# Shared keys of a two-block network: high weights over both parts of the activations in one 512-column product

## The chip, the cores and the metric

The kernel runs on one core of one Trainium2 chip. The metric is the device time of a run in microseconds (us), lower is better. Names of engines: PE is TensorE (matrix products; PEld is its weight load), DVE is VectorE, ACT is ScalarE, POOL is GpSimd, SP issues most DMAs. PSUM is the memory that PE writes to, eight banks of 512 fp32 columns in each of 128 partitions; SBUF is the memory that the engines work from.

## The reference, cut to what matters

Two blocks of two layers each run over 256 tokens of width 1024. The change touches one step of the second block, which makes the keys and values that a later attention layer uses:

```python
def _shared_kv(x, kv_norm, w_kv, k_gain):
    kv = (_rms(x, kv_norm) @ w_kv).reshape(bsz, seq, 2, B_GROUPS, B_HEADS, B_HEAD_DIM)
    k = _rms(kv[:, :, 0], k_gain[:, None, :])     # 3 groups x 16 heads x 64
    v = kv[:, :, 1]
```

That is a product of [256 x 1024] with [1024 x 6144], of which 3072 columns are keys, with a second normalisation over each head's 64 channels, and 3072 are values. All is fp32.

## The kernel before, in words

**Products in two parts.** Every fp32 weight and activation is split into a high and a low part of a type that PE multiplies in one pass (fp32r). ACT copies the weight to `hi` (L339), and DVE or POOL subtracts to get `lo` (L345). Activations are held as `xh` and `xl`. `product` (L393 to L397) adds three matmuls into PSUM: high weight x high activation, high x low, low x high.

**Chunks.** Weights come in chunks of 1024 x 256 through a ring of three buffers, so `hi` of chunk n can be written only when the products of chunk n-3 are done. Stages follow one another in one list (`PLAN`). The stage here is `kv`, between the feed-forward blocks `glu1` and `glu2`. It has 24 chunks, which alternate: chunk 2k holds keys and chunk 2k+1 values (k from 0 to 11). I call chunks 2k and 2k+1 pair k. `lo` of key chunks is made by DVE and `lo` of value chunks by POOL.

**A key chunk** is 2 halves of 128 output channels x 8 slices of the contraction x 3 matmuls of 256 columns (the tokens), 48 matmuls, all into one bank. **A value chunk** has the parts the other way round (activations are loaded, weights stream), 48 matmuls of 256 columns as well.

**What happens to the keys of pair k.** In this order: DVE multiplies the bank by the first normalisation's factors (L2268, raises `lin`). ACT squares (L2322, raises `sqr`). PE averages the squares over each head by an fp32 matmul with a constant (`mean`, L2224), placed between the two halves of value chunk 2k+1 for k > 0. ACT takes Ln (L2285) and Exp (L2288), each behind a table load. DVE scales the keys (L2260).

**The orders on the engines are written out by hand.** An engine works strictly down its list:

- ACT, turn k: square k, `hi` of 2k+3, Ln k, Exp k, the values of pair k out of their bank (L2293), `hi` of 2k+4, square k+1.
- DVE, turn k: `lo` of 2k+2, the keys of pair k out of their bank (L2268), scale keys k (L2260); for k = 6, 7, 8 also one addition for a table of position biases (L2277). Then `lo` of 2k+4.
- PE, pair k: key chunk, first half of the value chunk, mean k, second half; for k = 6, 7, 8 then a small matmul for the bias table (L2245).

At the end of the stage `glu2` needs new `xh` and `xl` (L1060 on ACT, L947 on DVE), since its gains differ. DVE makes `lo` of `glu2`'s second chunk first, then `xl`. PE's first matmul of `glu2` waits for the first two tiles of `xl`.

Of the kernel before, what the change touches and what calls it, by code (L numbers as in the profile page):

```python
# [132 lines left out]
def build(nc, A, out, plan=PLAN):  # L133

    ctx = ExitStack()
    with ctx:
        names = [0]

        def sb(name, shape, dt=F32):
            return ctx.enter_context(nc.sbuf_tensor(name, shape, dt))  # L140

        def sem(name):
            return ctx.enter_context(nc.semaphore(name))
# [3 lines left out]
        x = sb("x", [P, KT, T])  # L147
        hi = [sb(f"hi{i}", [P, 2048], F32R) for i in range(RING)]
        lo = [sb(f"lo{i}", [P, 2048], F32R) for i in range(RING)]
        xh = sb("xh", [P, KT, T], F32R)  # L150
        xl = sb("xl", [P, KT, T], F32R)
        gh = sb("gh", [P, 2, 2, T], F32R)
        gl = sb("gl", [P, 2, 2, T], F32R)
        cum_r, sel_r = sb("cum_r", [P, T], F32R), sb("sel_r", [P, 16], F32R)
# [6 lines left out]
        mean_d = sb("mean_d", [P, P])  # L161
        zero16 = sb("zero16", [1, P], BF16)
        ident = sb("ident", [P, P])
        bank = [ctx.enter_context(nc.psum_tensor(f"bank{i}", [P, 512], F32)) for i in range(8)]

        arena_at = nc.sbuf_base
        arena = sb("arena", [P, ARENA])
# [4 lines left out]
        def take(*shape, at=None):  # L172

            n = int(np.prod(shape))
            o = top[0] if at is None else at
            top[0] = o + n
            assert top[0] <= ARENA, top[0]
            v = arena[:, o:o + n]
            if len(shape) == 2:
                return v.rearrange("p (a b) -> p a b", a=shape[0])  # L180
            if len(shape) == 3:
                return v.rearrange("p (a b c) -> p a b c", a=shape[0], b=shape[1])
            return v
# [206 lines left out]
        def slot(n, width=CW, of=None):  # L390
            return (ring if of is None else of)[n % RING][:, 0:KT * width].rearrange("p (k n) -> p k n", k=KT)
# [285 lines left out]
        def pe_stats(pe, b):  # L677

            st = info[b]["st"]
            pe.wait_ge(ssq_new, st)  # L680
            nc.tensor.matmul(bank[7][:, 0:T], mean_d[:, :], ssq[:, :], start=True, stop=True)
            nc.tensor.matmul(bank[7][:, T:T + 1], ssq[:, 0:P], mean_d[:, 0:1], start=True, stop=True)
            nc.tensor.matmul(bank[7][:, T + 1:T + 2], ssq[:, P:T], mean_d[:, 0:1], start=True,
                             stop=True).then_inc(stat_new, 1)
            if b == FINAL:
                pe.wait_ge(fin_dve, 3)
                nc.tensor.matmul(bank[6][:, 0:T], mean_d[:, :], fin_q, start=True, stop=True)
                nc.tensor.matmul(bank[6][:, T:T + 1], fin_q[:, 0:P], mean_d[:, 0:1], start=True, stop=True)
                nc.tensor.matmul(bank[6][:, T + 1:T + 2], fin_q[:, P:T], mean_d[:, 0:1], start=True,
                                 stop=True).then_inc(fin_stat, 1)  # L690

        def pe_half(pe, n, B, mode, h, width=CW, tiles=None, acts=None, freed=False, ks=range(KT)):

# [1508 lines left out]
        def make_kv():  # L2202
# [4 lines left out]
            n0 = info["kv"]["c0"]  # L2207
            lin, sqr, mean_ok, log_ok, rec_ok, done = (sem("kv_" + k) for k in ("lin", "sqr", "mean", "log", "rec", "done"))
            small_in, rel_mm, rel_ok, v_ok = sem("kv_small_in"), sem("kv_rel_mm"), sem("kv_rel_ok"), sem("kv_v")


            def pe_part(pe):
                for c in range(24):
                    k, value = divmod(c, 2)
                    if c >= 4:
                        pe.wait_ge(v_ok if value else lin, k - 1)

                    def mean():
                        if k == 0:
                            pe.wait_ge(const_in, 16)  # L2220
                        pe.wait_ge(sqr, k + 1)
                        if k >= 2:
                            pe.wait_ge(log_ok, k - 1)
                        nc.tensor.matmul(bank[4 + k % 2][:, :], C["block64"][:, :], tmp_sq[k % 2], start=True,  # L2224
                                         stop=True).then_inc(mean_ok, 1)

                    early = value and k > 0
                    if c == 0:
                        pe_first_chunk(pe, "kv", bank[0])
                    for h in range(2 if c else 0):  # L2230
                        if h and early:
                            mean()
                        pe_half(pe, n0 + c, bank[c % 4], "tm" if value else "fm", h, freed=c == 23)
                    if c == 0:
                        pe_stats(pe, "kv")
                    if value:
                        if not early:
                            mean()
                        if 6 <= k < 9:
                            g = k - 6  # L2240
                            if g == 0:
                                pe.wait_ge(small_in, 16 * 3)
                            if g == 2:
                                pe.wait_ge(rel_ok, 1)
                            nc.tensor.matmul(bank[6 + g % 2][0:16, 0:384], RB[0:32, 16 * g:16 * g + 16],  # L2245
                                             HOT[0:32, g, :], start=True, stop=True).then_inc(rel_mm, 1)
                pe.wait_ge(v_ok, 11)
                pe.wait_ge(lin, 12)
                pe.wait_ge(rel_ok, 3)
# [12 lines left out]
            def dve_part(dve):  # L2262
                rs2 = rs_b[:, :].unsqueeze(1).broadcast_to([P, 2, T])
                for k in range(12):
                    lo_until(dve, n0 + 2 * k + 2)
                    dve.wait_ge(chunk_mul, n0 + 2 * k + 1)
                    two = DK[:, 2 * k:2 * k + 2, :]
                    nc.vector.tensor_tensor(two, bank[2 * k % 4][:, :].rearrange("p (e t) -> p e t", e=2), rs2,  # L2268
                                            ALU.mult).then_inc(lin, 1)
                    lo_until(dve, n0 + 2 * k + 3)  # L2270
                    if k < 11:
                        scale_keys(dve, k)
                    if 6 <= k < 9:
                        g = k - 6
                        dve.wait_ge(small_in, 16 * 3)
                        dve.wait_ge(rel_mm, g + 1)
                        nc.vector.tensor_tensor(RV[0:16, g, :], bank[6 + g % 2][0:16, 0:384], RM[0:16, g, :],  # L2277
                                                ALU.add).then_inc(rel_ok, 1)
                lo_until(dve, n0 + 25)

# [9 lines left out]
            def values_out(act, k):  # L2290
                act.wait_ge(chunk_mul, n0 + 2 * k + 2)
                for t in range(2):
                    last = nc.scalar.activation(DV[:, t, k * CW:(k + 1) * CW],  # L2293
                                                bank[(2 * k + 1) % 4][:, t * CW:(t + 1) * CW], ACT.Copy, scale=rs_c[:, t:t + 1])
                last.then_inc(v_ok, 1)

            def finish(act, k):
# [471 lines left out]
```

## Time and profile before

| | us |
|---|---|
| median of 3 runs | 1966.73 |
| lowest, highest | 1966.43, 1970.43 |
| span of the profiled execution, first to last instruction | 1963.3 |
| PE busy | 1906.0 (97%) |
| DVE busy | 1198.9 (61%) |
| ACT busy | 979.1 (50%) |
| POOL busy | 120.6 (6%) |

For the profiled execution the page gives the span and no other time; that lies 3.4 us below the median of the three timed runs. In a row of the timeline the first number is the start in us from the beginning of the span, the second the busy time, and brackets hold the time the engine was idle before it and who ended that. PE's matmuls are pipelined, so their starts tell their pace, not their durations. A busy share of 97% is a share over the whole span, and tells nothing on what would end a wait in one stage.

### The profile page before, as it was taken

What the parts mean: (1) busy time and instruction counts of PE and PEld (TensorE: products, weight loads), DVE (VectorE), ACT (ScalarE), POOL (GpSimd) and SP (SyncE); (2) the same over time, 40 slices, a digit from 0 to 9 for tenths busy, and PEclk for the clock granted to TensorE, in tenths of its full rate; (3) what the DMA queues carried; (4) which work ended last, traced back from release to release, by engine and by line L of the source; (5) the groups of instructions that cost most, each with busy time, mean ns of one, the idle gap of its engine ahead of it and who ended that gap; (6) DMA issues with size and microseconds to landing.
All of it is one profiled execution on the core that took longest, in us unless ns stands there. A gap on an engine that the chain in (4) does not pass through costs nothing.

```text
span 1963.3 us, 36765 instructions
## 1 busy us (share of the span) xinstructions
PE 1906.0 (97%) x15832; PEld 1834.1 (93%) x15832; DVE 1198.9 (61%) x1396; ACT 979.1 (50%) x1158; POOL 120.6 (6%) x54
## 2 busy tenths in 40 slices
PE   7999999999999999999999999999999998999999
PEld 7879999898999999999999999899999987779999
DVE  6677666755766775558667555533655566646554
ACT  6365444545544453345455444776534356655433
POOL 0000000010000000000000000333000021220000
PEclk9999999999999999999999999999999999999999
DMA  6315444432545445554335555454555446435552
GB/s 264 129 47 182 184 181 154 182 132 106 188 177 188 176 155 178 185 182 162 108 108 198 188 178 176 161 174 156 194 174 189 172 167 174 109 96 189 190 173 105
DMA packets 57980, 320.57 MB, mean 163 GB/s; under 512 B 6144, under 2 KB 19536, under 8 KB 20752
## 3 DMA queue, kind: packets, MB, share of 16 engines
q1 hardware_dynamic: 55968, 314.76, 46.6%
q10 hardware_dynamic: 1904, 4.24, 0.6%
q8 instruction: 84, 1.38, 0.3%
q14 instruction: 24, 0.20, 0.0%
HBM read 317.85 MB, written 1.12 MB: 162 GB/s over the span
## 4 chain that ended last, share of the span: by engine, by line
PE 85%; DVE 8%; ACT 4%; issue 2%; DMA 0%; SPq 0%; ACTq 0%; DVEq 0%
PE bank L395 26%; PE bank L396 25%; PE bank L397 25%; DVE lo L345 3%; ACT hi L339 2%; PE bank L462 1%; DVE xl L947 1%; PE bank L1884 1%; PE bank L499 1%; PE bank L2224 1%; DVE x L957 1%; PE bank L2389 1%; DMA ring<-in_ev_in 0%; PE bank L480 0%; DVE arena L555 0%
## 5 line engine op out<-in xcount | busy, mean ns | idle before, releaser
L395 PE MATMUL bank<-xh,hi 128*128 128x256 f32 x2960 | 848.7, 287 | 19.8 <-DVE lo L368 10.1
L396 PE MATMUL bank<-xl,hi 128*128 128x256 f32 x2960 | 841.4, 284 | 0.0
L397 PE MATMUL bank<-xh,lo 128*128 128x256 f32 x2960 | 841.2, 284 | 0.0
L345 DVE TENSOR_TENSOR lo<-ring,hi 128x2048 fp32r<-128x2048 f32 x272 | 619.6, 2283 | 306.2 <-ACT hi L339 305.9
L339 ACT ACTIVATE hi<-ring 128x2048 fp32r<-128x2048 f32 x290 | 549.2, 1898 | 424.7 <-PE bank L397 419.0
L395 PEld LDWEIGHTS bank<-xh,hi 128*128 128x128 f32 x2960 | 570.5, 193 | 29.3 <-issue 23.9
L396 PEld LDWEIGHTS bank<-xl,hi 128*128 128x128 f32 x2960 | 570.6, 193 | 1.8 <-issue 1.5
L397 PEld LDWEIGHTS bank<-xh,lo 128*128 128x128 f32 x2960 | 570.5, 193 | 0.3
L395 PE MATMUL bank<-gh,hi 128*128 128x256 f32 x1056 | 299.1, 283 | 2.1 <-DVE gl L877 2.1
L396 PE MATMUL bank<-gl,hi 128*128 128x256 f32 x1056 | 298.9, 283 | 0.0
L397 PE MATMUL bank<-gh,lo 128*128 128x256 f32 x1056 | 298.8, 283 | 0.0
L395 PEld LDWEIGHTS bank<-gh,hi 128*128 128x128 f32 x1056 | 202.7, 192 | 2.5 <-DVE gl L877 2.5
L397 PEld LDWEIGHTS bank<-gh,lo 128*128 128x128 f32 x1056 | 202.7, 192 | 0.0
L396 PEld LDWEIGHTS bank<-gl,hi 128*128 128x128 f32 x1056 | 202.7, 192 | 0.0
L345 POOL TENSOR_TENSOR lo<-ring,hi 128x2048 fp32r<-128x2048 f32 x18 | 84.7, 4707 | 1506.1 <-ACT hi L339 1506.1
L395 PE MATMUL bank<-hi,xh 128*128 128x256 f32 x368 | 110.0, 299 | 0.9 <-DVE arena L1669 0.8
L396 PE MATMUL bank<-lo,xh 128*128 128x256 f32 x368 | 104.0, 283 | 0.0
L397 PE MATMUL bank<-hi,xl 128*128 128x256 f32 x368 | 104.0, 283 | 0.0
L908 ACT ACTIVATE gh<-arena 128x512 fp32r<-128x512 f32 x66 | 41.7, 632 | 121.1 <-DVE arena L874 121.1
L845 DVE TENSOR_TENSOR arena<-bank,rs_b 128x512 f32<-128x512 f32 x66 | 45.6, 691 | 88.2 <-PE bank L397 88.0
L555 DVE TENSOR_TENSOR arena<-bank,arena 128x384 f32<-128x384 f32 x80 | 40.8, 551 | 65.9 <-PE bank L482 33.1
L395 PE MATMUL bank<-dk_r,hi 128*128 128x256 f32 x256 | 74.4, 291 | 2.3 <-DVE dk_r L594 2.0
(266 smaller groups left out, 1942.6 us busy)
## 6 DMA issues: line engine op xcount, KB each, us to landing
ring<-in_ffn_in SPq DMA_DIRECT2D x132, 1024.0 KB, 4.9
ring<-in_ffn_out SPq DMA_DIRECT2D x66, 1024.0 KB, 4.8
ring<-in_kv SPq DMA_DIRECT2D x24, 1024.0 KB, 4.9
ring<-in_hg_in SPq DMA_DIRECT2D x16, 1024.0 KB, 4.9
ring<-in_od_in SPq DMA_DIRECT2D x12, 1024.0 KB, 4.8
ring<-in_dq SPq DMA_DIRECT2D x12, 1024.0 KB, 4.9
ring<-in_ev_in SPq DMA_DIRECT2D x10, 1024.0 KB, 6.7
arena<-rel_rows SPq DMA_DIRECT2D x24, 256.0 KB, 3.7
```

The lines of the kernel that those rows point to most:

```text
L339: nc.scalar.activation(hi[n % RING][:, 0:words[n]], ring[n % RING][:, 0:words[n]], ACT.Copy).then_inc(hi_ok, 1)
L345: ns.tensor_tensor(lo[n % RING][:, 0:w], ring[n % RING][:, 0:w], hi[n % RING][:, 0:w].bitcast(F32), ALU.subtract).then_inc(lo_ok[lo_by[n]], 1)
L395: nc.tensor.matmul(out_, lh, rh, start=start, stop=False, **kw)
L396: nc.tensor.matmul(out_, lh, rl, start=False, stop=False, **kw)
L397: return nc.tensor.matmul(out_, ll, rh, start=False, stop=stop, **kw)
L462: last = nc.tensor.matmul(soft_bank(w, e)[:, c0:c1], sub["q"][:, q0:q0 + P], sub["k"][:, 0:k1], start=True, stop=one)
L499: nc.tensor.matmul(out[e][:, 0:T], un["subs"][e][g]["v"][0], s.pt[w % 2][e][:, 0:T], start=un["first"] and g == 0, stop=False, skip_group_ ...
L555: nc.vector.tensor_tensor(a[e][:, g, :], soft_bank(w, e)[:, 0:384], un["subs"][e][g]["add"], ALU.add).then_inc(soft_sem["masked"], 1)
L845: nc.vector.tensor_tensor(dst, ga, rs2, ALU.mult).then_inc(ff_read, 1)
L908: nc.scalar.activation(gh[:, par, :, :], ff_g[:, par, :, :], ACT.Copy).then_inc(gh_ok, 1)
L947: last = nc.vector.scalar_tensor_tensor(xl[:, t, :], x[:, t, :], gain_of(b, t), xh[:, t, :].bitcast(F32), ALU.mult, ALU.subtract)
L957: nc.vector.scalar_tensor_tensor(xs, y, scale, xs, ALU.mult, ALU.add).then_inc(x_new, 1)
```

## The change

In key chunks 1 to 11 (k > 0) the high weight is no longer run over `xh` and `xl` in two matmuls of 256 columns, but once over both, which now lie side by side in one tensor `xhl`. The result fills a whole bank of 512 columns: the first half is high x high (to which low x high is added), the second is high x low. Each of the two channel halves takes a bank of its own. DVE then copies the second halves to SBUF, adds the first halves to them, and multiplies the sum by the factors as before. Key chunk 0 and all value chunks keep their products. Banks are dealt out anew: keys in banks 0 and 1 (k even) or 6 and 7 (k odd), values in 2 and 3, and the bias table shares banks 4 and 5 with the means, for which PE's waits on `log_ok` and `rel_ok` are added. A wait on `std_new` stands ahead of chunk 2, since banks 6 and 7 are then written for the first time after the statistics in bank 7 were read.

```diff
-        xh = sb("xh", [P, KT, T], F32R)
-        xl = sb("xl", [P, KT, T], F32R)
+        xhl = sb("xhl", [P, 2, KT, T], F32R)
+        xh, xl = xhl[:, 0, :, :], xhl[:, 1, :, :]
...
+        def product_beside(B, lh, ll, both, start, stop):
+            nc.tensor.matmul(B[:, :].rearrange("p (l t) -> p l t", l=2), lh, both, start=start, stop=False)
+            return nc.tensor.matmul(B[:, 0:T], ll, both[:, 0, :], start=False, stop=stop)
...
+            low_half = take(2, T)
+            def rel_bank(g):
+                return bank[4 + (g + 1) % 2]
+            def key_banks(k):
+                return (0, 1) if k % 2 == 0 else (6, 7)
+            def key_halves(k):
+                a, b = key_banks(k)
+                two = banks[:, a:b + 1, :].rearrange("p e (l t) -> p l e t", l=2)
+                return two[:, 0, :, :], two[:, 1, :, :]
 
             def pe_part(pe):
                 for c in range(24):
...
+                    if c == 2:
+                        pe.wait_ge(std_new, info["kv"]["st"])
...
+                        if 7 <= k < 10:
+                            pe.wait_ge(rel_ok, k - 6)
...
-                        pe_half(pe, n0 + c, bank[c % 4], "tm" if value else "fm", h, freed=c == 23)
+                        if value:
+                            pe_half(pe, n0 + c, bank[2 + k % 2], "tm", h, freed=c == 23)
+                            continue
+                        if h == 0:
+                            wait_split(pe, n0 + c)
+                        wh, wl = slot(n0 + c, of=hi), slot(n0 + c, of=lo)
+                        e = slice(h * P, (h + 1) * P)
+                        for i in range(KT):
+                            last = product_beside(bank[key_banks(k)[h]], wh[:, i, e], wl[:, i, e], xhl[:, :, i, :],
+                                                  i == 0, i == KT - 1)
+                        if h == 1:
+                            last.then_inc(chunk_mul, 1)
...
-                            if g == 2:
-                                pe.wait_ge(rel_ok, 1)
+                            pe.wait_ge(log_ok, k)
...
                     two = DK[:, 2 * k:2 * k + 2, :]
-                    nc.vector.tensor_tensor(two, bank[2 * k % 4][:, :].rearrange("p (e t) -> p e t", e=2), rs2,
-                                            ALU.mult).then_inc(lin, 1)
+                    if k == 0:
+                        y = bank[0][:, :].rearrange("p (e t) -> p e t", e=2)
+                    else:
+                        main, side = key_halves(k)
+                        nc.vector.tensor_copy(low_half[:, :, :], side).then_inc(beside, 1)
+                        dve.wait_ge(beside, k)
+                        nc.vector.tensor_tensor(two, main, low_half[:, :, :], ALU.add).then_inc(joined, 1)
+                        dve.wait_ge(joined, k)
+                        y = two
+                    nc.vector.tensor_tensor(two, y, rs2, ALU.mult).then_inc(lin, 1)
```

What stands on DVE's list, in the `kv` stage from scale keys 0 to scale keys 1, before (L345 is `lo`, L2268 takes the keys out, L2260 scales them):

```order
841 L2260 SCALAR_TENSOR_TENSOR arena<-arena,vecs 128x512 [waits kv_rec]
842 L345 TENSOR_TENSOR lo<-ring,hi 128x2048 [waits hi_ok]
843 L2268 TENSOR_TENSOR arena<-bank,rs_b 128x512 [waits chunk_mul]
844 L2260 SCALAR_TENSOR_TENSOR arena<-arena,vecs 128x512 [waits kv_rec]
845 L345 TENSOR_TENSOR lo<-ring,hi 128x2048 [waits hi_ok]
```

The same place on DVE after the change (L346 is `lo`, L2304 the copy, L2306 the addition, L2309 the multiplication, L2292 the scaling):

```order
841 L2292 SCALAR_TENSOR_TENSOR arena<-arena,vecs 128x512 [waits kv_rec]
842 L346 TENSOR_TENSOR lo<-ring,hi 128x2048 [waits hi_ok]
843 L2304 COPY arena<-bank 128x512 [waits chunk_mul]
844 L2306 TENSOR_TENSOR arena<-bank,arena 128x512 [waits kv_beside]
845 L2309 TENSOR_TENSOR arena<-arena,rs_b 128x512 [waits kv_joined]
846 L2292 SCALAR_TENSOR_TENSOR arena<-arena,vecs 128x512 [waits kv_rec]
```

Nothing is moved past anything else: one instruction has become three, each behind the one before, between `lo` and the scaling. ACT's list is the same before and after.

PE's list at the seam from value chunk 3 to key chunk 4, before (L395 to L397 are `product`):

```order
6001 L397 MATMUL bank<-hi,xl 128x256
6002 L395 MATMUL bank<-xh,hi 128x256 [waits lo_ok_v,kv_lin]
6003 L396 MATMUL bank<-xl,hi 128x256
6004 L397 MATMUL bank<-xh,lo 128x256
6005 L395 MATMUL bank<-xh,hi 128x256
6006 L396 MATMUL bank<-xl,hi 128x256
```

The same seam on PE after the change (L695 and L696 are `product_beside`):

```order
5985 L398 MATMUL bank<-hi,xhl 128x256
5986 L695 MATMUL bank<-xhl,hi 128x512 [waits lo_ok_v,kv_lin]
5987 L696 MATMUL bank<-xhl,lo 128x256
5988 L695 MATMUL bank<-xhl,hi 128x512
5989 L696 MATMUL bank<-xhl,lo 128x256
```

Three matmuls of 256 columns have become one of 512 and one of 256, so a key chunk has 32 matmuls in place of 48 and as many columns.

## Rows read from the trace of the kernel before

**Rows 1.** Windows: busy us of PE, PEld, DVE, ACT, POOL, clock, DMA.
```profile
1298.00:1310.00 12.00, 12.00 (x97) 11.52 (x97) 4.24 (x3) 8.48 (x10) 4.61 (x1) 1.00 0.48 171
```

**Rows 2.** Timeline of ACT, 1253 to 1266: start, us, engine, line.
```profile
1253.80 0.63 ACT L2322 ACTIVATE arena<-arena 128x512 f32<-128x512 f32 x1 [2.96 <-DVE arena L2268]
1254.34 1.90 ACT L339 ACTIVATE hi<-ring 128x2048 fp32r<-128x2048 f32 x1
1256.25 1.28 ACT L2285 ACT_TABLE_LOAD   x1
1257.55 0.69 ACT L2285 ACTIVATE arena<-bank,eps_c 128x512 f32<-128x512 f32 x1
1258.25 1.28 ACT L2288 ACT_TABLE_LOAD   x1
...
1260.08 0.82 ACT L2293 ACTIVATE arena<-bank,rs_c 128x256 f32<-128x256 f32 x2
1260.80 1.91 ACT L339 ACTIVATE hi<-ring 128x2048 fp32r<-128x2048 f32 x1
1265.66 0.63 ACT L2322 ACTIVATE arena<-arena 128x512 f32<-128x512 f32 x1 [2.96 <-DVE arena L2268]
```

**Rows 3.** Timeline of DVE in the same stretch.
```profile
1262.74 2.29 DVE L345 TENSOR_TENSOR lo<-ring,hi 128x2048 fp32r<-128x2048 f32 x1 [1.26 <-ACT hi L339]
1264.94 0.68 DVE L2268 TENSOR_TENSOR arena<-bank,rs_b 128x512 f32<-128x512 f32 x1
```

**Rows 4.** Timeline of PE about the mean of pair 1.
```profile
1253.88 0.28 PE L396 MATMUL bank<-lo,xh 128*128 128x256 f32 x1
...
1254.00 0.28 PE L397 MATMUL bank<-hi,xl 128*128 128x256 f32 x1
...
1254.48 1.13 PE L2224 MATMUL bank<-arena 128*128 128x512 f32 x2 [0.20 <-ACT arena L2322]
...
1255.57 0.28 PE L396 MATMUL bank<-lo,xh 128*128 128x256 f32 x1
```

**Rows 5.** Waits, 1239 to 1383: us in total, times, longest.
```profile
ACT arena L2322 <- DVE arena L2268: 41.9, 12, 4.4
...
DVE arena L2268 <- PE bank L397: 6.0, 8, 1.4
```

**Rows 6.** Timeline of ACT and PE: squares of pairs 7 and 11, mean 11.
```profile
1327.80 0.63 ACT L2322 ACTIVATE arena<-arena 128x512 f32<-128x512 f32 x1 [4.40 <-DVE arena L2268]
...
1379.14 0.63 ACT L2322 ACTIVATE arena<-arena 128x512 f32<-128x512 f32 x1 [3.46 <-DVE arena L2268]
...
1381.10 1.02 PE L2224 MATMUL bank<-arena 128*128 128x512 f32 x2
```

**Rows 7.** Groups by line and form, DVE: count, busy us in all, mean ns.
```profile
L980 DVE TENSOR_TENSOR arena<-arena 128x512 f32<-128x512 f32 x10 | 6.9, 692 | 0.3
...
L1300 DVE COPY arena<-bank 15x128 f32<-15x128 f32 x1 | 0.3, 271 | 0.0
```

**Rows 8.** Timeline of DVE, an instruction behind the one that feeds it.
```profile
1235.43 1.23 DVE L978 TENSOR_TENSOR arena<-arena 128x1024 f32<-128x1024 f32 x1 [1.20 <-ACT arena L1068]
1236.69 0.69 DVE L980 TENSOR_TENSOR arena<-arena 128x512 f32<-128x512 f32 x1
```

**Rows 9.** Timeline, seam to `glu2`: DVE's `lo` and `xl`, PE's first matmul.
```profile
1381.61 2.29 DVE L345 TENSOR_TENSOR lo<-ring,hi 128x2048 fp32r<-128x2048 f32 x1 [2.50 <-ACT hi L339]
1383.88 3.28 DVE L947 SCALAR_TENSOR_TENSOR xl<-x,vecs,xh 128x256 fp32r<-128x256 f32 x8
...
1384.90 0.35 PE L395 MATMUL bank<-xh,hi 128*128 128x256 f32 x1
```

**Rows 10.** Windows about a fall of the clock.
```profile
380.00:382.00 2.00, 0.96 (x5) 0.96 (x6) 0.96 (x2) 2.00 (x3) 2.00 (x1) 0.83 0.52 119
382.00:384.00 2.00, 2.00 (x12) 2.00 (x11) 1.71 (x1) 0.19 (x1) 2.00 (x1) 0.50 0.93 393
```

**Rows 11.** Windows in `glu2`.
```profile
1410.00:1430.00 20.00, 20.00 (x169) 20.00 (x169) 11.66 (x8) 7.90 (x7) 0.00 (x0) 1.00 0.57 201
```

More of the change, by code:

```diff
@@ L163, in build @@
         ident = sb("ident", [P, P])
-        bank = [ctx.enter_context(nc.psum_tensor(f"bank{i}", [P, 512], F32)) for i in range(8)]
+        banks = ctx.enter_context(nc.psum_tensor("bank", [P, 8, 512], F32))
+        bank = [banks[:, i, :] for i in range(8)]
         arena_at = nc.sbuf_base
@@ L2209, in make_kv @@
             small_in, rel_mm, rel_ok, v_ok = sem("kv_small_in"), sem("kv_rel_mm"), sem("kv_rel_ok"), sem("kv_v")
+            beside, joined = sem("kv_beside"), sem("kv_joined")
+            low_half = take(2, T)
[7 more added lines that the diff above has]
+                return two[:, 0, :, :], two[:, 1, :, :]
             def pe_part(pe):
@@ L2242, in pe_part @@
                                 pe.wait_ge(small_in, 16 * 3)
-                            if g == 2:
-                                pe.wait_ge(rel_ok, 1)
-                            nc.tensor.matmul(bank[6 + g % 2][0:16, 0:384], RB[0:32, 16 * g:16 * g + 16],
+                            pe.wait_ge(log_ok, k)
+                            nc.tensor.matmul(rel_bank(g)[0:16, 0:384], RB[0:32, 16 * g:16 * g + 16],
                                              HOT[0:32, g, :], start=True, stop=True).then_inc(rel_mm, 1)
@@ L2276, in dve_part @@
                         dve.wait_ge(rel_mm, g + 1)
-                        nc.vector.tensor_tensor(RV[0:16, g, :], bank[6 + g % 2][0:16, 0:384], RM[0:16, g, :],
+                        nc.vector.tensor_tensor(RV[0:16, g, :], rel_bank(g)[0:16, 0:384], RM[0:16, g, :],
                                                 ALU.add).then_inc(rel_ok, 1)
@@ L2293, in values_out @@
                     last = nc.scalar.activation(DV[:, t, k * CW:(k + 1) * CW],
-                                                bank[(2 * k + 1) % 4][:, t * CW:(t + 1) * CW], ACT.Copy, scale=rs_c[:, t:t + 1])
+                                                bank[2 + k % 2][:, t * CW:(t + 1) * CW], ACT.Copy, scale=rs_c[:, t:t + 1])
                 last.then_inc(v_ok, 1)
```

## The prediction

> **What bounds the kernel now.** I read the page first. PE is busy nearly everywhere, so a change that takes work off PE looks good, but what it is worth depends on what ends the last wait in its stage. I therefore read the `kv` stage by itself. Its windows show PE busy 12.00 of 12.00 us, with DVE and ACT at 4.24 and 8.48 [rows 1]. Here PE sets the pace. The reader is to see next how far the others are behind it.
>
> The waits of the stage give that. ACT waits for DVE's L2268 twelve times, 41.9 us in all, and DVE in turn waits for PE at L2268 only 8 times, 6.0 us [rows 5]. So most of ACT's wait isn't PE's doing: it is DVE's own `lo` and L2268 that ACT sits behind. That is a loop of two engines. The timeline of pair 1 to pair 2 shows it where PE isn't in it. ACT runs from the square at 1253.80 without a gap through `hi`, table load, Ln, table load, Exp, the values and `hi` again, to 1260.80 + 1.91 = 1262.71 [rows 2]. DVE's `lo` waits for that `hi` and starts at 1262.74, L2268 follows at 1264.94 to 1265.62 [rows 3], and the next square starts at 1265.66 [rows 2]. One turn is 1265.66 - 1253.80 = 11.86 us, ACT's 8.91 and DVE's 2.92 with two handovers. No part of a turn can pass another, because each engine's list is strict and each handover is waited for.
>
> PE's turn is a little longer. A matmul of 256 columns starts each 0.12 us (1253.88, 1254.00) [rows 4], so a pair takes 96 x 0.12 = 11.52, and a mean some 0.85 more: 12.37. The rows agree: ACT idles 2.96 before a square where the loop is tight, and 3.46 or 4.40 where PE is later [rows 2, 6]. The loop's slack is thus 0.50 us in a plain pair, and 1.44 in the three pairs with a bias matmul. In all, ten turns from square 1 (1253.80) to square 11 (1379.14) take 125.34 us, and ten bare loops 118.6. The slack of the whole stage is 6.74 us [rows 2, 6].
>
> **PE's part of the change.** Eleven key chunks lose 16 matmuls each and keep their columns. [...] No row shows fp32r at 512 columns, so both sides are open. [...] Above: the two passes of the fp32 mean, 512 columns each, take (1255.57 - 0.12) - 1254.48 = 0.97 us with a cold start [rows 4], so at most 0.49 for 512 columns in place of 0.24, which is 4.0 us more a chunk. [...]
>
> **DVE's part.** L2268 becomes three instructions in a row. The multiplication stays at 0.69: the same form between SBUF operands, L980, takes 692 ns [rows 7]. The addition reads a bank and SBUF like L2268 itself, 0.68 [rows 3], so 0.69. The copy out of the bank has no row of its size. Lower end: the copy of 128 elements takes 0.271 [rows 7] and one of 512 can't be shorter. Upper end: 0.75, a little over the other forms of 128x512. I take 0.69, from the row of the same size and source. Between dependent instructions on DVE lie 1236.69 - (1235.43 + 1.23) = 0.03 us [rows 8], twice. Added per turn: 0.69 + 0.69 + 2 x 0.035 = 1.45 us, with ends 0.27 + 0.69 + 0.07 = 1.03 and 0.75 + 0.75 + 0.1 = 1.6.
>
> [...]
>
> **Where these 1.45 us lie.** Nothing hides them. They stand on DVE between `lo` and `lin`. Behind `lin` ACT's square is queued, and behind the square `hi` of the next value chunk, Ln, Exp, the values and the next `hi`, which DVE's next `lo` waits for. They therefore lengthen the loop: 11.86 + 1.45 = 13.31 us a turn, more than PE's 12.37, so the slack of 6.74 is used up and the loop sets the end. `lo` of key chunks stands on the same path, and nobody else makes it.
>
> The sum, from square 1 to square 11: the first join is already behind `lo` in the kernel before, so all 1.45 us count at square 1, and then ten turns of 13.31. Squares start at 1255.25 and 1255.25 + 133.1 = 1388.35, against 1379.14: **+9.2 us**. As a formula, 11 x (added per turn) - 6.74.
>
> PE must keep up for this to hold. It waits for the square before each mean. [...] DVE comes to the join 11.86 - 0.72 = 11.14 after it. [...]
>
> **The seam to `glu2`.** After square 11 ACT makes a `hi`, DVE its `lo` (1381.61 to 1383.90), then `xl` from 1383.88, and PE's first matmul of `glu2` follows the first two tiles of `xl` at 1384.90 [rows 9]. DVE's `lo` there hangs on the `hi` directly behind the square, so `xl` moves by the same 9.2, and PE with it. Before, PE had a mean late by 1.3 us behind its square (1379.14 + 0.63 to 1381.10, [rows 6]) as reserve; that reserve is gone too. In `glu2` PE is busy 20.00 of 20.00 [rows 11], so nothing is given back.
>
> **Edits at nothing.** The wait on `std_new` before chunk 2: ACT's read of bank 7 comes before the first key's factors, and value chunk 1 runs between. If that cover failed, PE would stand in pair 1, where it already waits for square 1. The waits on `log_ok` and `rel_ok`: Ln k stands 3.75 + 0.69 = 4.44 us behind square k [rows 2], and PE reaches the bias matmul 0.68 + 0.97 + 2.88 = 4.53 behind it. If it came later, the bias pairs would pay that difference. The new banks only change which buffers wait, at the same distance.
>
> **The sum.** Against the profiled execution: span 1963.3 + 9.2 = 1972.5. That span lies 3.4 below the median, so the median becomes 1966.7 + 9.2 = **1975.9 us**. The ends of the price per turn give 11 x 1.03 - 6.74 = +4.6 and 11 x 1.6 - 6.74 = +10.9, that is 1971.3 to 1977.6.
>
> **Rivals.**
>
> 1. *The join hides beside PE* (9%). One looks only at the 1.33 us between the end of square 11 and mean 11 and sets 1.45 against it. [...] For it: PE was the pace maker in nine of ten turns. Against: it forgets that the delay is handed on by ACT's list, and the turn of 11.86 us is there in the trace.
> 2. *PE's shorter key chunks show* (3%), the other side. [...] It decides from a price per turn of under 6.74 / 11 = 0.61 us; with three instructions in place of one, each over 0.27, only a `lo` that starts earlier could bring this. [...] No row shows it, and it needs the same condition on the loop; I give it 1 of the 3 in 100.
> 3. *The clock falls in PE's new gaps* (10%). [...] Elsewhere a stretch with PE busy 0.96 of 2 us is where the granted clock fell to 0.50, and 12 matmuls ran in the next 2 us where 17 do at 1.00 [rows 10, 11]. [...] Against: after the short stop before mean 1 the matmuls run on each 0.12.
> 4. *512 columns of fp32r are slow* (4%). At 0.49 us each, eleven chunks cost 44 us, PE is the bound and the gain of the loop's slack is off: about 2011.
>
> My forecast has the remaining 74%.
>
> **How the numbers follow.** No change is within 0.2%, about 3.9 us, which is what this kernel's measurement can tell. Faster is rival 2 at the page's rate and a little of its doubt: 0.03. Within 0.2%: rival 1, the rest of rival 2, and the lowest tail of the forecast: 0.09. Slower: 0.88. The range of 1971.5 to 1980 holds the forecast's own range and most of rival 3.
>
> **What would show it.** Right: squares (`lin` to `sqr`) start 13.3 us apart in pairs 1 to 11, ACT's idle time before a square is about 4.4 in all of them, DVE's wait for PE at the join is near nothing, PE idles about 1 us before means of plain pairs, and `glu2` starts 9 us late. The copy's row shows 0.69. Wrong: squares 12.4 apart; a copy near 0.3; PE waiting nowhere; key chunks other than 5.5 us; a granted clock of 0.50 in the stage.

## The result and the profile after

| | before | after |
|---|---|---|
| median, us | 1966.58 (6 runs) | 1975.11 (6 runs) |
| ratio of after to before, 95% interval | | 1.0044 [1.0033, 1.0055] |
| span of the profiled execution, us | 1963.3 | 1971.3 |

The ratio is +8.6 us, with an interval of +6.5 to +10.8. The forecast was +9.2 and 1975.9. One of the six runs after took 4658 us, as one of e1 below took 9233 and one of e2 2044; they are left out of the ratios, and nothing below explains them.

The timeline of ACT after the change, the first turn of the loop (start, busy us, engine, line; in brackets the idle time before and who ended it), answers to [rows 2]:

```profile
1258.39 0.63 ACT L2362 ACTIVATE arena<-arena 128x512 f32<-128x512 f32 x1 [4.41 <-DVE arena L2309]
1258.93 1.89 ACT L340 ACTIVATE hi<-ring 128x2048 fp32r<-128x2048 f32 x1
...
1262.14 0.69 ACT L2325 ACTIVATE arena<-bank,eps_c 128x512 f32<-128x512 f32 x1
...
1265.39 1.91 ACT L340 ACTIVATE hi<-ring 128x2048 fp32r<-128x2048 f32 x1
1271.71 0.63 ACT L2362 ACTIVATE arena<-arena 128x512 f32<-128x512 f32 x1 [4.41 <-DVE arena L2309]
```

The timeline of DVE in the same stretch, for [rows 3]:

```profile
1267.33 2.29 DVE L346 TENSOR_TENSOR lo<-ring,hi 128x2048 fp32r<-128x2048 f32 x1 [1.27 <-ACT hi L340]
1269.54 0.68 DVE L2304 COPY arena<-bank 128x512 f32<-128x512 f32 x1
1270.26 0.69 DVE L2306 TENSOR_TENSOR arena<-bank,arena 128x512 f32<-128x512 f32 x1
1270.98 0.69 DVE L2309 TENSOR_TENSOR arena<-arena,rs_b 128x512 f32<-128x512 f32 x1
```

ACT's own work is unchanged (8.91 us from the square's start to the end of the second `hi`, 1265.39 + 1.91 = 1267.30). DVE's `lo` starts 0.03 behind it, the join follows without a gap, and the square follows the join. One turn is 1271.71 - 1258.39 = 13.32 us, where it was 11.86 [rows 2].

The waits of the stage after the change (us in all, times, longest), for [rows 5]:

```profile
ACT arena L2362 <- DVE arena L2309: 51.7, 12, 4.6
...
PEld bank L2246 <- ACT arena L2362: 9.8, 11, 2.1
PE bank L2246 <- ACT arena L2362: 7.4, 8, 1.9
```

ACT's wait for the keys grew from 41.9 to 51.7. DVE's wait for PE (6.0 before) is gone from the list. In its place PE's weight load waits for the square at 11 means, and PE itself at 8 of them. That is how a change of the bound looks: the row of waiting for PE disappears, and a row in which PE waits takes its place.

The timeline of PE, inside key chunk 4 and about mean 1, for [rows 4]:

```profile
1265.03 0.40 PE L695 MATMUL bank<-xhl,hi 128*128 128x512 f32 x1
1265.26 0.28 PE L696 MATMUL bank<-xhl,lo 128*128 128x256 f32 x1
1265.38 0.40 PE L695 MATMUL bank<-xhl,hi 128*128 128x512 f32 x1
```
```profile
1256.92 0.28 PE L398 MATMUL bank<-hi,xhl 128*128 128x256 f32 x1
1259.08 1.12 PE L2246 MATMUL bank<-arena 128*128 128x512 f32 x2 [1.88 <-ACT arena L2362]
```

From one L695 to the next it is 0.35 us (9 of them from 1265.03 to 1268.21 give 0.353), against 0.36 for three matmuls before. So a matmul of 512 columns of fp32r takes about twice the 0.12 us of one of 256 (0.353 less 0.12, 0.233), and a key chunk saves 16 x 0.007 = 0.11 us. PE then stands 1.9 us at mean 1. At seven of the other means the profile books 0.8 us idle (by the starts it is 0.95: 1.07 from the last matmul to the mean, less the usual 0.12), and none at the three behind a bias matmul. Mean 3:

```profile
1284.64 0.28 PE L398 MATMUL bank<-hi,xhl 128*128 128x256 f32 x1
1285.71 1.12 PE L2246 MATMUL bank<-arena 128*128 128x512 f32 x2 [0.79 <-ACT arena L2362]
```

The seam to `glu2` after the change, for [rows 9]: `lo` and `xl` on DVE, then PE's first matmul.

```profile
1394.54 2.29 DVE L346 TENSOR_TENSOR lo<-ring,hi 128x2048 fp32r<-128x2048 f32 x1 [2.50 <-ACT hi L340]
1396.75 3.25 DVE L953 SCALAR_TENSOR_TENSOR xhl<-x,vecs,xhl 128x256 fp32r<-128x256 f32 x8
```
```profile
1397.77 0.36 PE L396 MATMUL bank<-xhl,hi 128*128 128x256 f32 x1 [1.03 <-DVE xhl L953]
```

**A measure of the stage.** For the comparisons below I take, in each trace, the time from the start of the sum of squares on DVE ahead of the stage (the 128x512 addition, 1236.69 in [rows 8]) to PE's first matmul of `glu2` (1384.90 in [rows 9]): **148.21 us before**. After the change the first of them is

```profile
1239.82 0.69 DVE L986 TENSOR_TENSOR arena<-arena 128x512 f32<-128x512 f32 x1
```

and the stage is 1397.77 - 1239.82 = **157.95 us, +9.74**.

**Where the rest of the span goes.** The stage begins 3.1 us later after the change, and what follows it is 4.9 us shorter (573.5 against 578.4), so the span differs by 8.0. Neither is work that the change added. Both go with where the granted clock falls to 0.50 for a while: ahead of the stage for 17.1 us after the change against 10.2 before, behind it for 3.4 us against 17.1 (a fall at the very end of each span left out). The last attention stage shows it. The same place of the program lies 12.9 us later after the change: the DVE addition of 128x512 ahead of it starts at 1583.48 before and at 1596.35 after. The windows of before and then of after, over that place (bounds and length in us, busy PE, PEld, DVE, ACT, POOL, clock, DMA share, GB/s):

```profile
1584.00:1588.00 4.00, 3.32 (x20) 3.27 (x21) 3.04 (x5) 3.70 (x4) 2.14 (x1) 0.78 0.06 16
```
```profile
1596.90:1600.90 4.00, 3.35 (x26) 3.30 (x27) 3.04 (x5) 3.67 (x4) 2.17 (x1) 1.00 0.06 16
```

DVE, ACT and POOL do the same work in both, to 0.03 us; PE gets through 20 matmuls at the clock of 0.78 and 26 at 1.00.

The experiments mostly say the same. Behind the stage the traces with 3.4 us at the low level take 573.5 and 574.6, the four with 6.8 take 575.0 to 575.2, one with 10.2 takes 577.0, one with 13.6 takes 578.0, and the four with 17.1 take 577.5 to 579.2. That the change has no part in where the clock falls is not shown: behind the stage the four traces of kernels with the old products take 577.0 to 579.2 us, the eight with the new ones 573.5 to 578.0.

### The profile page after: what moved, and what is told of

It is laid out like the page before. It is cut to its first block, busy times and chain, and to the rows that moved or that the text cites. A ratio compares the mean times of both kernels' runs of the same rounds, so it can differ in the third digit from the quotient of the medians.

```text
span 1971.3 us, 36437 instructions
## 1 busy us (share of the span) xinstructions
PE 1904.0 (97%) x15656; PEld 1823.1 (92%) x15656; DVE 1213.3 (62%) x1418; ACT 978.8 (50%) x1158; POOL 120.7 (6%) x54
## 4 chain that ended last, share of the span: by engine, by line
PE 78%; DVE 10%; ACT 8%; issue 3%; DMA 1%; SPq 0%; ACTq 0%; DVEq 0%
PE bank L396 24%; PE bank L398 23%; PE bank L397 23%; DVE lo L346 4%; ACT hi L340 3%; PE bank L463 1%; DVE xhl L953 1%; PE bank L1890 1%; PE bank L500 1%; PE bank L695 1%; DVE x L963 1%; DVE arena L556 1%; DMA ring<-in_ev_in 0%; PE bank L481 0%; ACT L2325 0%
## 5 line engine op out<-in xcount | busy, mean ns | idle before, releaser
L396 PE MATMUL bank<-xhl,hi 128*128 128x256 f32 x2784 | 798.2, 287 | 20.4 <-DVE lo L369 9.8
L346 DVE TENSOR_TENSOR lo<-ring,hi 128x2048 fp32r<-128x2048 f32 x272 | 619.6, 2283 | 308.1 <-ACT hi L340 308.0
L397 PE MATMUL bank<-xhl,hi 128*128 128x256 f32 x2784 | 791.5, 284 | 0.0
L398 PE MATMUL bank<-xhl,lo 128*128 128x256 f32 x2784 | 791.2, 284 | 0.0
L396 PEld LDWEIGHTS bank<-xhl,hi 128*128 128x128 f32 x2784 | 536.5, 193 | 27.4 <-issue 22.1
L397 PEld LDWEIGHTS bank<-xhl,hi 128*128 128x128 f32 x2784 | 536.7, 193 | 1.5 <-issue 1.3
L398 PEld LDWEIGHTS bank<-xhl,lo 128*128 128x128 f32 x2784 | 536.5, 193 | 0.3
L397 PE MATMUL bank<-gl,hi 128*128 128x256 f32 x1056 | 299.0, 283 | 0.0
L397 PEld LDWEIGHTS bank<-gl,hi 128*128 128x128 f32 x1056 | 202.8, 192 | 0.0
L346 POOL TENSOR_TENSOR lo<-ring,hi 128x2048 fp32r<-128x2048 f32 x18 | 84.8, 4711 | 1518.9 <-ACT hi L340 1518.9
L396 PE MATMUL bank<-hi,xhl 128*128 128x256 f32 x368 | 110.0, 299 | 0.9 <-DVE arena L1675 0.8
L397 PE MATMUL bank<-lo,xhl 128*128 128x256 f32 x368 | 104.1, 283 | 0.0
L398 PE MATMUL bank<-hi,xhl 128*128 128x256 f32 x368 | 104.0, 283 | 0.0
```

Of the source, the lines that this page charges most:

```text
L346: ns.tensor_tensor(lo[n % RING][:, 0:w], ring[n % RING][:, 0:w], hi[n % RING][:, 0:w].bitcast(F32), ALU.subtract).then_inc(lo_ok[lo_by[n]], 1)
L396: nc.tensor.matmul(out_, lh, rh, start=start, stop=False, **kw)
L397: nc.tensor.matmul(out_, lh, rl, start=False, stop=False, **kw)
L398: return nc.tensor.matmul(out_, ll, rh, start=False, stop=stop, **kw)
```

## The experiments

Two theories stood at first. A: a loop of ACT and DVE sets the end, and DVE's two new instructions lie in it. B: what costs is on PE, in the 512-column matmuls or in the banks and waits dealt out anew. Each table row below is from the run's own trace: the measured stage, the distance of squares in a plain pair and in a bias pair, and the ratio against before.

| run | stage, us | plain turn | bias turn | ratio [95%] |
|---|---|---|---|---|
| before | 148.21 | 12.37 | 13.30 | |
| after | 157.95 | 13.32 | 13.48 | 1.0044 [1.0033, 1.0055] |
| e1: before, two DVE instructions more | 158.20 | 13.32 | 13.58 | 1.0049 [1.0033, 1.0066] |
| e2: before, one more | 151.15 | 12.59 | 13.30 | 1.0018 [1.0008, 1.0028] |
| e3: after, no join | 147.17 | 12.27 | 13.20 | 0.9982 [0.9973, 0.9992] |
| e4: after, one more | 165.92 | 14.05 | 14.20 | 1.0096 [1.0079, 1.0113] |
| e5: after, `lo` behind the join | 150.69 | 12.54 | 13.48 | 1.0008 [0.9998, 1.0018] |
| e6, e10: e5 with the join in halves | 147.07 | 12.26 | 13.20 | 0.9983, 0.9987 [0.9977, 0.9996] |
| e7: after, copy on ACT | 152.09 | 12.60 | 13.46 | 1.0014 [1.0005, 1.0024] |
| e8: before, `lo` behind | 148.59, less 0.83 | 12.37 | 13.30 | 0.9990 [0.9980, 0.9999] |
| e9: halves, `lo` ahead | 163.36, less 0.86 | 13.78 | 13.78 | 1.0063 [1.0048, 1.0079] |

A turn in the table is that of the settled stage. Before and e3 begin with two and three turns of 11.86 to 11.89, the bare loop, and e2's first bias turn is 12.87.

In e8 and e9 the granted clock fell to 0.50 at about 1233.5 for 3.4 us, just ahead of the stage. PE's matmuls of 256 columns start each 0.21 us there in place of 0.12 and end later, ACT's next `hi` waits 0.89 us for its buffer, and the square roots of the statistics stand behind it on ACT's list: DVE waits for them 1.94 us in e8 where it waited 0.92 before, and square 0 comes 7.93 and 7.92 us after the stage's start in place of 6.91. That delay isn't of the kernel. The rows are ACT's `hi` in e8, then DVE in e8 and in before:

```profile
1239.88 1.92 ACT L339 ACTIVATE hi<-ring 128x2048 fp32r<-128x2048 f32 x1 [0.89 <-PE bank L397]
```
```profile
1243.77 0.17 DVE L1013 RECIPROCAL rs_c<-std_c 128x2 f32<-128x2 f32 x1 [1.94 <-ACT arena L1076]
```
```profile
1240.97 0.17 DVE L1013 RECIPROCAL rs_c<-std_c 128x2 f32<-128x2 f32 x1 [0.92 <-ACT arena L1076]
```

Not all of it reaches the end of the stage, since before PE came to mean 0 only 0.4 us after its square had ended. In e8, where PE sets the pace, what counts is when PE is through mean 0: the second matmul behind it starts 9.75 us after the stage's start, where it was 8.92, so 0.83 us later. The rows are PE's in e8 and in before:

```profile
1248.22 0.28 PE L396 MATMUL bank<-xl,hi 128*128 128x256 f32 x1
```
```profile
1245.61 0.28 PE L396 MATMUL bank<-xl,hi 128*128 128x256 f32 x1
```

In e9, where the loop sets the pace, square 1 starts 19.89 us after the stage's start; 17.11 of before and the price of 1.92 found below make 19.03, so 0.86. I take these off.

**e1: DVE's part alone.**

```diff
+                    y = bank[2 * k % 4][:, :].rearrange("p (e t) -> p e t", e=2)
+                    if k > 0:
+                        nc.vector.tensor_copy(low_half[:, :, :], y).then_inc(beside, 1)
+                        dve.wait_ge(beside, k)
+                        nc.vector.tensor_tensor(two, y, low_half[:, :, :], ALU.add).then_inc(joined, 1)
+                        dve.wait_ge(joined, k)
```

> The kernel before, with its matmuls and banks as they were. In pairs 1 to 11 DVE does a copy of the key bank (128x512) into a scratch tensor and an addition of bank and scratch ahead of its multiplication, the same three instructions in a row as after the change; the multiplication still reads the bank, so the keys are unchanged. Theory A (the loop of ACT and DVE sets the end, the matmuls don't matter): the stage from DVE's sum of squares (TENSOR_TENSOR of 128x512 behind that of 128x1024) to PE's first matmul of glu2 is 9.7 us longer than before's 148.2, so 157.9, squares 13.3 apart, time +9 us. Rival B (what costs is the 512-column matmul, or the new banks and waits on PE): stage within 1 us of before, time +0 to +1 us.

Its timeline of DVE:

```profile
1269.07 2.29 DVE L345 TENSOR_TENSOR lo<-ring,hi 128x2048 fp32r<-128x2048 f32 x1 [1.26 <-ACT hi L339]
1271.28 0.68 DVE L2272 COPY arena<-bank 128x512 f32<-128x512 f32 x1
1272.00 0.69 DVE L2274 TENSOR_TENSOR arena<-bank,arena 128x512 f32<-128x512 f32 x1
1272.72 0.69 DVE L2276 TENSOR_TENSOR arena<-bank,rs_b 128x512 f32<-128x512 f32 x1
```

Stage 158.20, squares 13.32 apart, without one 512-column matmul. This is the whole loss, and 0.25 more (its bias turns are 13.58, PE having the longer key chunks). B falls.

**e3: PE's part alone.** The low part of the activations is left out of the keys here.

```diff
-                        nc.vector.tensor_copy(low_half[:, :, :], side).then_inc(beside, 1)
-                        dve.wait_ge(beside, k)
-                        nc.vector.tensor_tensor(two, main, low_half[:, :, :], ALU.add).then_inc(joined, 1)
-                        dve.wait_ge(joined, k)
-                        y = two
+                        y = main
```

> The changed kernel without the copy and the addition: DVE multiplies the first halves of the two banks alone, so the product of high weights with the low part of the activations is computed but left out of the keys. Theory A: the loop is back at 11.86 us, PE sets the pace again at its own, 16 x 0.007 = 0.11 us shorter per key chunk by the pace seen after the change (0.353 for 512 + 256 columns against 0.360 for three times 256): stage 148.2 - 11 x 0.11 = 147.0, time -1 us against before. Rival B (the matmuls or the new banks cost): stage over 150. [...]

Its waits show the picture of before again, with DVE waiting for PE:

```profile
ACT arena L2358 <- DVE arena L2305: 40.8, 12, 4.3
DVE lo L346 <- ACT hi L340: 15.7, 12, 2.5
DVE arena L2305 <- PE bank L696: 4.9, 7, 1.2
```

Stage 147.17, 1.04 us less than before, turn 12.27 in place of 12.37. The matmuls, banks and waits together bring 0.1 us a pair, as the pace said; a cost of theirs doesn't show.

**e2 and e4: one instruction more on either side of the bend.** e2 is e1 without the addition. e4 adds to the changed kernel:

```diff
+                        nc.vector.tensor_copy(low_half[:, :, :], side).then_inc(again, 1)
+                        dve.wait_ge(again, k)
```

> The kernel before with one more DVE instruction per pair, the copy of 128x512 into a scratch tensor, price 0.72 us per turn. Theory A gives 11 x 0.72 - 6.74 = +1.2 us, since the slack of the loop takes up most of it: stage 149.4 to 150. Rival C (each DVE microsecond counts alike, as if DVE were simply on the path): 11 x 0.72 = +7.9 us, stage 156. Squares: A says 12.58 us apart in plain pairs where before has 12.37, and 13.3 in the three bias pairs as before.

> The changed kernel with the copy done a second time behind the addition: one more DVE instruction in the row, 0.72 us per turn. Theory A: no slack is left, so all of it counts: 11 x 0.72 = +7.9 us on the changed kernel, stage 157.95 + 7.9 = 165.9, squares 14.0 apart everywhere. Together with the one of e2 (+1.2) this is the bend in the curve. Rival C (each DVE microsecond counts alike, with no bend): the same +7.9 here but also +7.9 in e2. Rival D (PE's stop before the mean is what sets the turn, and DVE's extra time is partly beside it): +4 or less.

e4 came to 165.92, on the number: where no slack is left each 0.72 us counts in full, and D falls with it. e2 came to 151.15, +2.9 and not +1.2. Theory C (+7.9) falls, and the plain turns are 12.59 as A says, but my formula was wrong for this price. It spends all 6.74 us of slack, and part of that lies in the bias pairs, 1.44 each, of which a price of 0.72 uses only half. Turn by turn it works: +0.73 at square 1 and then the longer of loop and PE in each turn, 12.59 or 13.3. The first bias turn of e2 is 12.87, since until then the loop had set the pace and PE had its key chunk ready before DVE came for it. PE's extra 0.94 us first used up that lead, some 0.66, and only the remaining 0.28 lengthened the turn.

**e5, e9, e6: is it the work or its place?** e5 moves one line of DVE's list:

```diff
-                    lo_until(dve, n0 + 2 * k + 2)
                     dve.wait_ge(chunk_mul, n0 + 2 * k + 1)
...
                     nc.vector.tensor_tensor(two, y, rs2, ALU.mult).then_inc(lin, 1)
+                    lo_until(dve, n0 + 2 * k + 2)
```

> The changed kernel, with DVE's lo of chunk 2k+2 moved behind the join of pair k, nothing else. Theory A: lo (2.29 us) leaves the path from ACT's hi to the square, so the loop is 8.91 + 2.15 + handovers = 11.1 us and no longer sets the pace. What is left: square k ends 0.2 + 2.11 + 0.07 + 0.63 = 3.0 us after the key chunk, and PE wants the mean after 2.88, so PE stops 0.1 to 0.3 in each pair: stage 148.2 - 1.2 + 11 x 0.2 = 149 to 150.5, time +1 to +2 us against before. Rival E (the join costs what it takes wherever it stands): stage stays near 158.

Stage 150.69: 7.3 of the 9.7 us are back with the same instructions on every engine. Its waits name the new order: DVE now waits for PE (30.6 us), because it comes to the join before the key chunk is done.

```profile
ACT arena L2362 <- DVE arena L2308: 44.4, 12, 4.6
DVE arena L2303 <- PE bank L696: 30.6, 11, 3.2
```

What is left is 12.54 - 12.27 = 0.27 a turn, PE's stop before the mean, and a wait of 1.02 us for `xl` at the seam. e6 takes the stop away by cutting the join in two:

```diff
+                        for e in range(2):
+                            if e == 0:
+                                dve.wait_ge(half_mul, k)
+                            else:
+                                dve.wait_ge(chunk_mul, n0 + 2 * k + 1)
+                            one, B1, s1 = DK[:, 2 * k + e, :], bank[key_banks(k)[e]], low_half[:, e, :]
+                            nc.vector.tensor_copy(s1, B1[:, T:2 * T]).then_inc(beside, 1)
+                            dve.wait_ge(beside, 2 * k - 1 + e)
+                            nc.vector.tensor_tensor(one, B1[:, 0:T], s1, ALU.add).then_inc(joined, 1)
+                            dve.wait_ge(joined, 2 * k - 1 + e)
+                            last = nc.vector.tensor_tensor(one, one, rs_b[:, :], ALU.mult)
...
-                        if h == 1:
-                            last.then_inc(chunk_mul, 1)
+                        last.then_inc(chunk_mul if h else half_mul, 1)
```

> The changed kernel with lo behind the join, and the join cut in two: the first channel half is copied, added and multiplied (128x256 each) while PE computes the second, on a semaphore of its own. After the chunk's end three instructions of 0.42 are left, 1.3 us in place of 2.1, so square k ends 2.2 us after the key chunk and PE's mean, 2.88 after it, doesn't wait. Theory A: PE sets the pace in all pairs, stage 148.2 - 1.2 = 147.0, time -1.2 us against before. Rival E: near 158 or above, since DVE does more work (2.5 us a pair in place of 2.1).

The timeline of DVE in e6:

```profile
1274.27 0.42 DVE L2308 COPY arena<-bank 128x256 f32<-128x256 f32 x1 [0.40 <-PE bank L696]
1274.73 0.42 DVE L2310 TENSOR_TENSOR arena<-bank,arena 128x256 f32<-128x256 f32 x1
1275.19 0.42 DVE L2312 TENSOR_TENSOR arena<-arena,rs_b 128x256 f32<-128x256 f32 x1
1277.09 0.42 DVE L2308 COPY arena<-bank 128x256 f32<-128x256 f32 x1 [1.48 <-PE bank L696]
1277.55 0.42 DVE L2310 TENSOR_TENSOR arena<-bank,arena 128x256 f32<-128x256 f32 x1
1278.01 0.42 DVE L2312 TENSOR_TENSOR arena<-arena,rs_b 128x256 f32<-128x256 f32 x1
1278.35 2.28 DVE L346 TENSOR_TENSOR lo<-ring,hi 128x2048 fp32r<-128x2048 f32 x1
```

The first half is done 1.48 us before the second can start. Stage 147.07, turn 12.26, as with no join at all. (The stages of e3 and e6 each keep one stop: 0.43 us at mean 1 in e3, 0.50 at the seam in e6.) e9 is e6 with `lo` ahead of the join again:

> The join cut in two as in e6, with lo of chunk 2k+2 ahead of it again as in the changed kernel. It tells whether e6 owes its time to the cut or to the place of lo. Theory A: lo ends 11.2 us into the turn, when the first half's bank has long been complete, so all six instructions of 128x256 (0.42 each, 0.035 between dependent ones) stand behind it in the loop: 2.6 us in place of before's 0.69, price 1.9 a turn, 11 x 1.9 - 6.74 = +14 us, stage 162, squares 13.7 to 13.8 apart. Rival F (the cut by itself hides the first half beside PE, wherever lo stands): stage 148 to 155.

Stage 162.50 without the delay ahead of it, for an expected 162, and all turns 13.78, the bias pairs included; only e4 is slower. The price is 1.92 a turn (13.78 - 11.86). The cut alone hides nothing, because both halves stand behind `lo`. Rival F falls.

**e7: the copy on ACT, in its idle time.**

```diff
-                        nc.vector.tensor_copy(low_half[:, :, :], side).then_inc(beside, 1)
...
+                    if k > 0:
+                        act.wait_ge(chunk_mul, n0 + 2 * k + 1)
+                        nc.scalar.activation(low_half[:, :, :], key_halves(k)[1], ACT.Copy).then_inc(beside, 1)
                     act.wait_ge(lin, k + 1)
```

> The changed kernel with ACT making the copy of the second halves, ahead of its wait for lin, in the idle time before the square; DVE adds and multiplies. lo stays ahead of the join. Theory A: in plain pairs the key chunk ends at about 10.1 of the turn, ACT's copy runs until 10.9 and DVE comes to the join at 11.14, so the price per turn is 0.72 there, turn 12.58. In the three bias pairs PE is 0.94 later, and ACT's copy until 11.8 delays DVE by 0.7: turn 13.3. Stage 148.2 + 1.2 + up to 2 = 149.5 to 151.5, time +1.5 to +3 us against before. Rival C: the copy costs the same on ACT as on DVE, since both stand in one loop: stage 158.

```profile
1266.15 0.60 ACT L2360 ACTIVATE arena<-bank 128x512 f32<-128x512 f32 x1 [1.46 <-PE bank L696]
1268.38 0.63 ACT L2364 ACTIVATE arena<-arena 128x512 f32<-128x512 f32 x1 [1.62 <-DVE arena L2308]
```

ACT copies in 0.60 and then idles 1.62 more until the square, so the copy is free there and the plain turn is 12.60, that of one added DVE instruction. In the bias pairs it isn't free, since DVE waits for it:

```profile
1330.77 0.69 DVE L2305 TENSOR_TENSOR arena<-bank,arena 128x512 f32<-128x512 f32 x1 [0.77 <-ACT arena L2360]
```

Those turns are 13.46. The stage of 152.09 lies 0.6 over my upper figure, again because the slack of the bias pairs isn't there for the plain ones. Rival C (158) falls.

**e8: the other order in the kernel before.** The same line moved as in e5.

> The kernel before with DVE's lo of chunk 2k+2 moved behind the taking out of the keys of pair k. Theory A: PE sets the pace already, so only the first turns gain, where the loop was tight and mean 1 waited 0.2 to 0.5 us for its square: stage 147.6 to 148.2, time -0.3 us at most. If it were more than 1 us faster, the slack of the loop wasn't what I read.

The turns from square 1 on are all 12.37 or, in the bias pairs, 13.30, so PE sets the pace from the start, and the stage is 147.76 without the delay ahead of it: 0.45 us less than before, within the range expected for the stage, though a little more than the 0.3 I had as the most. The ratio of 0.9990 is -2.0 us, but its interval reaches -0.2, so it is no measure of half a microsecond. The order that brings 7.3 us after the change brings some 0.45 before it.

**e10: e6 once more.**

> The kernel of e6 once more, in more rounds, to size it against before: the stage is 1.1 us shorter in e6's trace (147.07 against 148.21), so a ratio of 0.9994 is expected if the rest of the kernel is the same, and the interval should reach up to it. e6's own ratio of 0.9983 was more than that. Rival G (something outside the stage also got faster, such as the products of other stages with the activations side by side in one tensor): 0.998 again, with other stages shorter in the trace at a granted clock of 1.00 throughout.

Ratio 0.9987 [0.9977, 0.9996], median 1963.31 against 1966.23, stage 147.07 again. The stage accounts for 1.1 us, 0.0006, and the interval reaches 0.9996, not 0.9994. Rival G doesn't show in the long stages at clock 1.00 either. The windows of before and then of e10:

```profile
720.00:1200.00 480.00, 476.57 (x4261) 469.03 (x4260) 291.00 (x276) 214.74 (x196) 0.00 (x0) 1.00 0.49 167
```
```profile
720.00:1200.00 480.00, 476.56 (x4261) 469.02 (x4260) 292.22 (x278) 214.74 (x196) 0.00 (x0) 1.00 0.49 168
```

As many matmuls in as much time. What the stage leaves open is 1.4 us in e10 and 2.2 in e6. In the traces e10 is 1.2 us longer ahead of the stage and 3.4 shorter behind it, 575.0 us against 578.4, with 6.8 us at the low clock against 17.1. The timed runs point the same way, with a mean granted clock of 0.9940 over the 11 runs of e10 and 0.9928 over the 15 of before; before alone spans 1963.15 to 1970.14 in these. That the places of the falls make up the rest is likely. Why e10 has fewer, and whether the new products have a share in it, is not shown.

## Why the prediction was right, point by point

**The loop of 11.86 us and its price.** Right. It was read from one pair in which PE wasn't late. (DVE's part of it is 2.88 with handovers of 0.03 and 0.04, not the 2.92 of the text; the 11.86 stand.) After the change every plain turn is 13.32, forecast 13.31. e1 has it without PE's part, e3 loses it without DVE's, e4 lengthens it by 0.73 for 0.72.

**The formula, 11 x (added per turn) - 6.74.** Right for this price, and that is partly luck. It spends the slack of all turns together, but the slack lies unevenly: none in the first two turns (11.86 and 11.87), 0.35 in the third, 0.5 in each of four more plain turns, and 1.44 in the three with a bias matmul. Only a price of 1.44 or more uses all of it, and 1.45 just does. For a smaller price the formula says too little: for 0.72 it gives +1.2, and e2 measured +2.9. By the same fault the lower end of the range, +4.6 from a price of 1.03, lay too low, and the limit of 0.61 us a turn that rival 2 was given lay too high. PE was the pace maker in eight of the ten turns, as [rows 5] say with their 8 waits, and not in nine.

**The durations.** Right. The copy has a median of 683 ns (0.69), addition and multiplication 691. By the two copies out of a bank, 271 ns for 128 elements and 683 for 512, an element more costs 1.07 ns.

**PE keeps up.** Right in kind: PE idles 0.95 us by its starts before the means of plain pairs, forecast about 1. Two sizes were off. I had looked for key chunks of 5.5 us (5.76 less 16 x 0.013), from a price of 0.013 us per matmul; that price was my own assumption, and no run shows it. The runs give an estimated 0.007: 3 x 256 columns take 0.360 and 512 + 256 take 0.353, so a chunk saves 0.11 and takes 5.65. And from a square's start to the end of the next key chunk I had counted 10.03 us for PE, where 0.63 for the square, 0.05 for the handover, 0.97 for the mean, 2.88 for half a chunk and 5.65 for the key chunk make 10.18. Because of both PE ended key chunks in the bias pairs a little later, and those turns are 13.48, not 13.31: 3 x 0.16 = 0.5 us, which is the difference between 9.2 and the 9.74 of the stage.

**The seam.** Right: `xl` starts 9.74 us later relative to the stage's start (156.93 against 147.19), and PE waits 1.03 us for it where it had been on time within 0.1.

**Edits at nothing.** Right, by e3: with all of them in place the stage is 1.04 us shorter than before.

**The rivals.** Rival 1 (hidden beside PE) fails by the mechanism it left out: ACT's list hands the delay on, which e5 takes away and finds 7.3 us. Rival 2 needs a lower price than any version with `lo` ahead of the join has: at 0.72 e2 and e7 are still slower than before. Its 1 in 100 for a faster matmul of 512 columns rested on a rate that no run shows: such a matmul takes 353 ns less one 256-column matmul of 113 to 120, so some 235. Rival 3: the granted clock stays at 1.00 in the whole stage after the change, with PE stopping 0.8 us in each plain turn and 1.9 at mean 1. The 1980 at the end of the range took in some 4 us for such falls, an estimate that rested on my price per matmul too, and no run shows them in the stage. Rival 4: 235 ns and not 490. One turn of the stage after the change, for rival 3:

```profile
1275.00:1288.30 13.30, 12.51 (x84) 11.08 (x83) 5.53 (x5) 8.83 (x10) 4.59 (x2) 1.00 0.46 158
```

**The time.** 1975.11 against 1975.9. The closeness is partly luck: single runs of one kernel differ by more than the half microsecond in which the stage itself was missed, those of before by 7 us (1963.15 at a mean granted clock of 0.994 to 1970.14 at 0.990).

## What to carry to other kernels

Before adding work to an engine that is 60% busy, look for the loop it stands in: follow who releases whom until you are back at the same instruction, in a turn where the busiest engine isn't late, and compare that turn with the busiest engine's. Here 0.5 us of slack stood between the two, and 1.45 us of additions turned the bound over. When slack differs from turn to turn, price each turn by itself and don't sum the slack: summed, it promised +1.2 us for e2, and +2.9 was measured. Ask also of each instruction in the loop whether it must be there: moving one independent 2.3 us instruction behind the handover gave back 7.3 of 9.7 us without removing anything, and cutting the new work so that half of it starts early gave back the rest.

## What the runs showed of the hardware

Of fp32r matmuls with 128 x 128 weights at the granted clock of 1.00, a price per instruction of only an estimated 7 ns beside 113 ns for 256 columns (worked out from 0.360 us for three matmuls of 256 columns and 0.353 for one of 512 and one of 256), though each loads its weights anew (97 loads beside 97 matmuls in [rows 1]). ACT copies 128x512 fp32 from PSUM in 0.60 us, DVE in 0.68. PE stood 1.9 us once and 0.8 us before each of seven means in the stage after the change with its granted clock at 1.00 throughout, while over 4 us at the same place of the last attention stage the clock was 0.78 in the trace of before and 1.00 in that of after. Where it was 0.50, ahead of the stage in e8, matmuls of 256 columns started each 0.21 us in place of 0.12.
